# A two-layer encoder on one core: giving every split-weight buffer its own start remainder modulo 512 bytes

## The chip, the core and the metric

The kernel runs on one core of a Trainium2 chip. Its engines work side by side and hand work to each other through semaphores: TensorE (PE in the views; PEld is its weight load), VectorE (DVE), ScalarE (ACT), GpSimd (POOL) and SyncE (SP), which issues the loads from device memory. SBUF is the on-chip memory from which they read their operands, 128 partitions wide; an address here is a byte offset along a partition. The metric is the device time of one execution in microseconds.

## What is computed

The reference is a trunk of two layers on an input of 512 tokens by 1024 features in float32. Cut to what matters:

```python
for i in range(2):
    h = rms_norm(x, mix_pre_g[i])
    if i == 0: m = ssd_mixer(h, ...)        # w_in (1024 x 6176), scan over chunks, w_out (2048 x 1024)
    else:      m = shortconv_mixer(h, ...)  # w_in (1024 x 3072), conv of 3, w_out (1024 x 1024)
    x = x + rms_norm(m, mix_post_g[i])
    f = conv_ffn(rms_norm(x, ffn_pre_g[i]), ...)   # w_up (1024 x 5632), conv of 3, w_down (2816 x 1024)
    x = x + rms_norm(f, ffn_post_g[i])
```

Nearly all of the arithmetic is in these matrix products.

## The kernel before

**Split operands.** Every large product is made of three matmuls in the type float32r. Each float32 operand is split into a high part and a low part (the rest), and the three products high x high, high x low, low x high are summed in one PSUM bank. The activations are kept in split form: `h_hi` and `h_lo`, `y_hi` and `y_lo`, `hid_hi` and `hid_lo`.

**Weight units.** The weights come in 228 units of 128 x 1024 elements, numbered `u`. SyncE loads a unit into one of two raw buffers `w_raw`. ScalarE copies it to `w_hi` (line 355), VectorE writes the difference to `w_lo` (line 585), and TensorE reads both. The function `splits_to(end)`, one on ScalarE and one on VectorE, does the splits up to a unit, and the calls to it are written by hand between the other work of the two engines. A unit's pair of buffers is a slot. The 48 units of the first layer's input product use three slots; from unit `U_OUT` = 48 on there are five, and the 180 units there take them in turn:

```python
def slot(u):
    return u % 3 if u < U_OUT else (u - U_OUT) % SLOTS
```

ScalarE may split unit `u` when the unit that had the slot before is done on TensorE (`before(u)`, semaphore `unit_done`). Slots 3 and 4 lie in memory that the first layer's scan used, so their first use waits for the scan instead: on `seg_done` for slot 3 and on `scan_done` for slot 4.

**Two ways of using a unit.** In the function `unit` (lines 849 to 851, through `three`) the weights are the stationary operand, 128 x 128 at a time, and the activations move through, 512 columns in one matmul; `half_unit` does the same with 256 columns, for three units after each of three of the four output products. In `project` (lines 910 to 912) the activations are stationary and 512 columns of the weights move. Either way one unit takes 24 matmuls of 512 columns (48 of 256 in a half unit), and every matmul has a weight load of its own. TensorE's order of work is fixed in its block and has no slack of its own.

**Where operands begin.** The tensors are allocated one behind another. The sizes of nearly all per partition are multiples of 512 bytes, and in the built program all the large operands (`x_tok`, `h_hi`, `h_lo`, `w_raw`, all ten `w_hi`/`w_lo`, `hid_hi`, `hid_lo`, `feat`, `pad`) begin at the same remainder modulo 512 bytes. The slices that TensorE takes of them are at multiples of 512 bytes too. VectorE's and ScalarE's accesses are not all so: the convolution reads `pad[:, f % 2, tap:tap + T]` for taps 0, 1 and 2 (line 645), thus at 0, 4 and 8 bytes past a multiple of 512, and ScalarE writes the same buffer from element 3 on (line 406), 12 bytes past one.

Other lines that the views name: 1013 are the transposes of `feat`, 1020 and 1038 the float32 matmuls of the scan with its state, 1030 those with the mask (the last that `scan_done` counts), 1060 a sum over partitions with one moving column. These are float32, without a split.

Of the kernel before, what the change touches and what calls it, by code (L numbers as in the profile page):

```python
# [6 lines left out]
F32R = mybir.dt.float32r  # L7
# [3 lines left out]
P = 128  # L11
# [4 lines left out]
def build(nc, x, mix_pre_g, mix_post_g, ffn_pre_g, ffn_post_g, ssd_w_in, ssd_conv_w, ssd_conv_b,  # L16
          ssd_dt_bias, ssd_A_log, ssd_D, ssd_norm_w, ssd_w_out, sc_w_in, sc_conv_w, sc_w_out,
          ffn_w_up, ffn_conv_w, ffn_conv_b, ffn_w_down, out):
    _, T, D = x.shape
# [6 lines left out]
    GROUPS = 8  # L26
# [76 lines left out]
    U_OUT = len(SOURCES)  # L103
# [18 lines left out]
    def slot(u):  # L122
        return u % 3 if u < U_OUT else (u - U_OUT) % SLOTS

    def before(u):

        if u < U_OUT + 3:
            return u - 3 if u >= 3 else None
        return u - SLOTS if u >= U_OUT + SLOTS else None
# [22 lines left out]
    with ctx:  # L152
        def sb(name, shape, dt=F32, stack=ctx):
            return stack.enter_context(nc.sbuf_tensor(name, shape, dt))

        def sem(name):
            return ctx.enter_context(nc.semaphore(name))
# [3 lines left out]
        x_tok = sb("x_tok", [P, C, D])  # L161
        h_hi, h_lo = sb("h_hi", [P, DT, T], F32R), sb("h_lo", [P, DT, T], F32R)
        w_raw = sb("w_raw", [P, 2, D])
        w_hi = [sb(f"w_hi{n}", [P, D], F32R) for n in range(3)]
        w_lo = [sb(f"w_lo{n}", [P, D], F32R) for n in range(3)]
        ident, tri = sb("ident", [P, P]), sb("tri", [P, P])
        par = sb("par", [P, 4, P])

# [43 lines left out]

        with ExitStack() as rest:

            for n in (3, 4):
                w_hi.append(sb(f"w_hi{n}", [P, D], F32R, rest))
                w_lo.append(sb(f"w_lo{n}", [P, D], F32R, rest))
            g_row = sb("g_row", [P, D], stack=rest)
            r_row = sb("r_row", [P, 2, T], stack=rest)

            with ExitStack() as at_boundary:
                scaled = sb("scaled", [P, 2, D], stack=at_boundary)
            cpad = sb("cpad", [P, T + P], stack=rest)
            acc, gated, side = (sb(n, [P, T], stack=rest) for n in ("acc", "gated", "side"))
            hid_hi, hid_lo = sb("hid_hi", [P, FT, T], F32R, rest), sb("hid_lo", [P, FT, T], F32R, rest)
# [17 lines left out]
        evicted, seg_done, exps_done, conv_step, silu_done = (  # L243
            sem(n) for n in ("evicted", "seg_done", "exps_done", "conv_step", "silu_done"))
# [97 lines left out]
        def _(act):  # L342
            split_at = [0]

            def splits_to(end):

                for u in range(split_at[0], min(end, U_END)):
                    act.wait_ge(raw_landed[u % 2], 16 * (u // 2 + 1))
                    if before(u) is not None:
                        act.wait_ge(unit_done, before(u) + 1)  # L350
                    elif u == U_OUT + 3:
                        act.wait_ge(seg_done, GROUPS)
                    elif u == U_OUT + 4:
                        act.wait_ge(scan_done, GROUPS)
                    nc.scalar.activation(w_hi[slot(u)][:], w_raw[:, u % 2, :], ACT.Copy).then_inc(w_hi_done, 1)  # L355
                    split_at[0] = u + 1
# [11 lines left out]
            for k in range(DT):  # L368
                act.wait_ge(xn_turned, k + 1)
                nc.scalar.activation(h_hi[:, k, :], bank[k % 6][:], ACT.Copy, scale=one(col_gain(MIX_PRE, 0, k))).then_inc(h0_hi_done, 1)  # L370
                if k == 0:
                    act.wait_ge(wdt_landed, 16)
                    act.wait_ge(wdt_cleared, 2)
                    nc.scalar.activation(wdt_hi[:, :, 0:HEADS], wdt_raw[:], ACT.Copy).then_inc(wdt_split, 1)
                if k == 3:
                    splits_to(1)
            splits_to(2)
            act.wait_ge(dt_row_mm, 1)
            nc.scalar.copy(dt_row[:], bank[7][0:HEADS, :]).then_inc(dt_row_done, 1)
# [11 lines left out]
            act.wait_ge(dt_act, 3)  # L391
            nc.scalar.activation(dt_e[:], dt_e[:], ACT.Ln, bias=1.0).then_inc(dt_act, 1)
            splits_to(3)
            act.wait_ge(acs_mm, 1)
            nc.scalar.copy(acs_row[:], bank[2][0:HEADS, :]).then_inc(acs_row_done, 1)
# [34 lines left out]
            for g in range(GROUPS):  # L430
# [25 lines left out]
                for j in range(XG):  # L456
                    n = XG * g + j
# [679 lines left out]
```

## Time and profile before

| | |
|---|---|
| median of three runs | 1345.62 us (1345.48 to 1346.71) |
| the profiled execution | 1345.41 us |
| its span, first to last instruction | 1343.7 us |
| PE busy | 1332.0 us, 99% |
| PEld busy | 1115.5 us, 83% |
| DVE busy | 784.3 us, 58% |
| ACT busy | 569.2 us, 42% |
| DMA | 101 GB/s on average |
| granted TensorE clock | 1.000 of full speed |

Busy shares are of the span. A matmul's record is longer than the step from one matmul's start to the next one's, since they are pipelined; so the duration of one is not what it costs. What it costs is the step between starts, called the pitch below.

### The profile page before, as it was taken

The numbers are of one execution on the slowest core, as the hardware profiler recorded it, in microseconds if no ns is written. First come the engines' busy times: TensorE is split into PE (matmuls) and PEld (weight loads), VectorE is DVE, ScalarE is ACT, GpSimd is POOL, SyncE is SP. The second block draws the span as 40 slices with busy tenths as digits, with TensorE's granted clock in tenths as the row PEclk, the third lists the DMA queues.
The fourth block names the chain that finished last, engine by engine and source line by source line (L and its number), as shares of the span: only waits on it lengthen the run. The fifth ranks groups of instructions, "written<-read, shape, count | busy, mean of one in ns | idle before, by whom it ended". The sixth has DMA issues, their size and how long they took to land.

```text
span 1343.7 us, 15929 instructions
## 1 busy us (share of the span) xinstructions
PE 1332.0 (99%) x6474; PEld 1115.5 (83%) x6474; DVE 784.3 (58%) x1139; ACT 569.2 (42%) x875; POOL 24.8 (2%) x28
## 2 busy tenths in 40 slices
PE   8999999999999999999999999999999999999998
PEld 7888888888888988888888888888898888888886
DVE  4889888888525566656542265445566666654223
ACT  6666655566316434333331173222554433333112
POOL 0000000000000000000000000000000000000000
PEclk9999999999999999999999999999999999999999
DMA  5533233432231233333333313334223333333331
GB/s 151 161 110 92 84 107 110 125 110 90 94 125 54 79 95 109 99 103 96 95 125 112 101 55 94 94 99 128 72 69 106 109 94 96 104 99 126 96 108 63
DMA packets 181773, 135.70 MB, mean 101 GB/s; under 512 B 5645, under 2 KB 169893, under 8 KB 180677
## 3 DMA queue, kind: packets, MB, share of 16 engines
q1 hardware_dynamic: 181653, 134.62, 32.8%
q8 instruction: 51, 0.84, 0.2%
q14 instruction: 21, 0.17, 0.0%
q10 hardware_dynamic: 48, 0.07, 0.0%
HBM read 132.51 MB, written 2.16 MB: 100 GB/s over the span
## 4 chain that ended last, share of the span: by engine, by line
PE 97%; ACT 1%; issue 0%; DVE 0%; DMA 0%; SPq 0%; DVEq 0%; ACTq 0%
PE bank L849 21%; PE bank L851 21%; PE bank L850 21%; PE bank L910 9%; PE bank L911 9%; PE bank L912 9%; PE bank L1030 1%; PE bank L1038 1%; PE bank L1020 1%; PE bank L887 1%; PE bank L1013 1%; PE bank L1002 0%; DMA pages<-in_ssd_norm_w 0%; ACT w_hi L355 0%; ACT h_hi L370 0%
## 5 line engine op out<-in xcount | busy, mean ns | idle before, releaser
L849 PE MATMUL bank<-h_hi,w_hi 128*128 128x512 f32 (+1 forms) x1352 | 513.8, 380 | 0.0
L851 PE MATMUL bank<-h_lo,w_hi 128*128 128x512 f32 (+1 forms) x1352 | 511.1, 378 | 0.0
L850 PE MATMUL bank<-h_hi,w_lo 128*128 128x512 f32 (+1 forms) x1352 | 510.8, 378 | 0.0
L585 DVE TENSOR_TENSOR w_lo<-w_raw,w_hi 128x1024 fp32r<-128x1024 f32 x228 | 286.0, 1257 | 325.8 <-ACT w_hi L355 325.8
L355 ACT ACTIVATE w_hi<-w_raw 128x1024 fp32r<-128x1024 f32 x228 | 238.4, 1053 | 195.3 <-PE bank L912 172.3
L851 PEld LDWEIGHTS bank<-h_lo,w_hi 128*128 128x128 f32 x1352 | 254.2, 188 | 47.4
L850 PEld LDWEIGHTS bank<-h_hi,w_lo 128*128 128x128 f32 x1352 | 254.4, 188 | 46.6
L849 PEld LDWEIGHTS bank<-h_hi,w_hi 128*128 128x128 f32 x1352 | 254.3, 188 | 46.4
L910 PE MATMUL bank<-w_hi,hid_hi 128*128 128x512 f32 x416 | 162.4, 390 | 0.0
L912 PE MATMUL bank<-w_hi,hid_lo 128*128 128x512 f32 x416 | 161.9, 389 | 0.0
L911 PE MATMUL bank<-w_lo,hid_hi 128*128 128x512 f32 x416 | 161.8, 389 | 0.0
L912 PEld LDWEIGHTS bank<-w_hi,hid_lo 128*128 128x128 f32 x416 | 78.1, 188 | 16.3
L910 PEld LDWEIGHTS bank<-w_hi,hid_hi 128*128 128x128 f32 x416 | 78.1, 188 | 16.1
L911 PEld LDWEIGHTS bank<-w_lo,hid_hi 128*128 128x128 f32 x416 | 78.1, 188 | 15.9
L780 DVE SCALAR_TENSOR_TENSOR acc<-cpad,par,acc 128x512 f32<-128x512 f32 x104 | 77.9, 749 | 4.4 <-ACT acc L542 1.8
L645 DVE SCALAR_TENSOR_TENSOR feat<-pad,par,feat 128x512 f32<-128x512 f32 x96 | 71.5, 751 | 13.6 <-ACT feat L407 11.3
L546 ACT ACTIVATE acc<-acc 128x512 f32<-128x512 f32 x44 | 27.9, 634 | 115.8 <-DVE acc L780 115.8
L542 ACT ACTIVATE acc<-cpad,par 128x512 f32<-128x512 f32 x44 | 35.9, 817 | 81.9 <-DVE cpad L793 81.9
L549 ACT ACTIVATE hid_hi<-gated 128x512 fp32r<-128x512 f32 x44 | 27.8, 633 | 81.2 <-DVE gated L802 81.2
L785 DVE TENSOR_TENSOR hid_lo<-gated,hid_hi 128x512 fp32r<-128x512 f32 x52 | 36.0, 693 | 36.4 <-ACT hid_hi L549 30.8
L910 PE MATMUL bank<-w_hi,y_hi 128*128 128x512 f32 x128 | 50.3, 393 | 0.0
L912 PE MATMUL bank<-w_hi,y_lo 128*128 128x512 f32 x128 | 49.9, 390 | 0.0
(146 smaller groups left out, 943.9 us busy)
## 6 DMA issues: line engine op xcount, KB each, us to landing
w_raw<-in_ffn_w_up SPq DMA_DIRECT2D x88, 512.0 KB, 3.7
w_raw<-in_ssd_w_in SPq DMA_DIRECT2D x48, 512.0 KB, 3.9
w_raw<-in_ffn_w_down SPq DMA_DIRECT2D x44, 512.0 KB, 3.5
w_raw<-in_sc_w_in SPq DMA_DIRECT2D x24, 512.0 KB, 3.7
acs_b<-acs_dram SPq DMA_DIRECT2D x8, 1024.0 KB, 6.1
w_raw<-in_ssd_w_out SPq DMA_DIRECT2D x16, 512.0 KB, 3.5
w_raw<-in_sc_w_out SPq DMA_DIRECT2D x8, 512.0 KB, 3.5
x_tok<-in_x SPq DMA_DIRECT2D x4, 512.0 KB, 4.9
```

The costliest lines, as they stand in the source:

```text
L355: nc.scalar.activation(w_hi[slot(u)][:], w_raw[:, u % 2, :], ACT.Copy).then_inc(w_hi_done, 1)
L542: nc.scalar.activation(acc[:], cpad[:, CW - 1:CW - 1 + T], ACT.Identity, bias=one(col_ffn_b(layer, t)), scale=one(col_ffn_w(layer, CW - 1, ...
L585: nc.vector.tensor_tensor(w_lo[slot(u)][:], w_raw[:, u % 2, :], w_hi[slot(u)][:].bitcast(F32), ALU.subtract).then_inc(w_lo_done, 1)
L645: nc.vector.scalar_tensor_tensor(out=feat[:, f, :], in0=pad[:, f % 2, tap:tap + T], scalar=one(col_ssd_w(tap, page_tile)), in1=feat[:, f, ...
L780: nc.vector.scalar_tensor_tensor(out=acc[:], in0=cpad[:, tap:tap + T], scalar=one(cols(tap)), in1=acc[:], op0=ALU.mult, op1=ALU.add).then_ ...
L785: nc.vector.tensor_tensor(hid_lo[:, t, :], gated[:], hid_hi[:, t, :].bitcast(F32), ALU.subtract).then_inc(hid_lo_done, 1)
L849: nc.tensor.matmul(dst, wh, xh, start=start, stop=False)
L850: nc.tensor.matmul(dst, wl, xh, start=False, stop=False)
L851: return nc.tensor.matmul(dst, wh, xl, start=False, stop=stop)
L910: nc.tensor.matmul(dst[:], in_hi[:, k, toks], hi, start=k == 0, stop=False)
L911: nc.tensor.matmul(dst[:], in_hi[:, k, toks], lo, start=False, stop=False)
L912: last = nc.tensor.matmul(dst[:], in_lo[:, k, toks], hi, start=False, stop=k == b.tiles - 1)
```

## The change

The buffers of the split weights are no longer tensors of their own but views into two larger tensors, `w_split` for slots 0 to 2 and `w_split_rest` for slots 3 and 4. A view is shifted by a number of bytes of its own, so that each of the ten parts begins at another remainder modulo 512 bytes, counted from the remainder at which the other operands begin:

| slot | high part | low part |
|---|---|---|
| 0 | 128 | 256 |
| 1 | 384 | 16 |
| 2 | 448 | 192 |
| 3 | 8 | 160 |
| 4 | 480 | 320 |

Each of the two tensors is 512 bytes longer than its parts, so all tensors behind them move by a multiple of 512 bytes and keep their remainders. With the shift the part of slot 4 reaches past the memory of the mask, and slot 3's low part into it, so slot 3's first use now waits on `scan_done` too.

```diff
-        w_hi = [sb(f"w_hi{n}", [P, D], F32R) for n in range(3)]
-        w_lo = [sb(f"w_lo{n}", [P, D], F32R) for n in range(3)]
+
+        w_split = sb("w_split", [P, 6 * D + P], F32R)
+
+        def part(src, nth, shift):
+            return src[:, nth * D + shift // 4:(nth + 1) * D + shift // 4]
+
+        w_hi = [part(w_split, 1, 128), part(w_split, 4, 384), part(w_split, 5, 448)]
+        w_lo = [part(w_split, 3, 256), part(w_split, 0, 16), part(w_split, 2, 192)]
...
-            for n in (3, 4):
-                w_hi.append(sb(f"w_hi{n}", [P, D], F32R, rest))
-                w_lo.append(sb(f"w_lo{n}", [P, D], F32R, rest))
+            w_split_rest = sb("w_split_rest", [P, 4 * D + P], F32R, rest)
+            w_hi += [part(w_split_rest, 0, 8), part(w_split_rest, 3, 480)]
+            w_lo += [part(w_split_rest, 1, 160), part(w_split_rest, 2, 320)]
...
-                    elif u == U_OUT + 3:
-                        act.wait_ge(seg_done, GROUPS)
-                    elif u == U_OUT + 4:
+                    elif u >= U_OUT + 3:
                         act.wait_ge(scan_done, GROUPS)
```

No engine gets an instruction more or less, and none changes its place. The one wait that changes stands in ScalarE's row at the end of the last scan group, where it has written the last two pieces of `y_hi` and their squares. Before:

```order
L459 ACTIVATE y_hi<-feat,par 128x512 [waits y_step]
L462 ACTIVATE square<-feat 128x512 [waits summed]
L355 ACTIVATE w_hi3<-w_raw 128x1024 [waits seg_done,raw_landed1]
L355 ACTIVATE w_hi4<-w_raw 128x1024 [waits scan_done,raw_landed0]
L562 ACTIVATE small<-bank5 128x4 [waits y_sum_mm]
```

And after the change, at the same place:

```order
L463 ACTIVATE y_hi<-feat,par 128x512 [waits y_step]
L466 ACTIVATE square<-feat 128x512 [waits summed]
L359 ACTIVATE w_split_rest<-w_raw 128x1024 [waits scan_done,raw_landed1]
L359 ACTIVATE w_split_rest<-w_raw 128x1024 [waits scan_done,raw_landed0]
L566 ACTIVATE small<-bank5 128x4 [waits y_sum_mm]
```

The rows stand as they stood; only the semaphore ahead of slot 3's first use is another, and all line numbers from there on are four or more higher.

## Rows read from the trace of the kernel before

**Rows 1.** The page: busy time of TensorE, and the chain that ended last.

```profile
PE 1332.0 (99%) x6474; PEld 1115.5 (83%) x6474; DVE 784.3 (58%) x1139; ACT 569.2 (42%) x875; POOL 24.8 (2%) x28
...
PE 97%; ACT 1%; issue 0%; DVE 0%; DMA 0%; SPq 0%; DVEq 0%; ACTq 0%
```

**Rows 2.** TensorE's waits, first and last of five: total us, times, longest.

```profile
PE bank L855 <- POOL tri L330: 1.8, 1, 1.8
...
PE bank L1013 <- ACT feat L413: 0.2, 1, 0.2
```

**Rows 3.** TensorE's groups by shape: count, busy us, mean ns, idle us before.

```profile
L849 PE MATMUL bank<-h_hi,w_hi 128*128 128x512 f32 x1208 | 472.8, 391 | 0.0
...
L910 PE MATMUL bank<-w_hi,hid_hi 128*128 128x512 f32 x416 | 162.4, 390 | 0.0
...
L910 PE MATMUL bank<-w_hi,y_hi 128*128 128x512 f32 x128 | 50.3, 393 | 0.0
...
L849 PE MATMUL bank<-h_hi,w_hi 128*128 128x256 f32 x144 | 41.0, 285 | 0.0
```

**Rows 4.** One stretch of 512-column matmuls: busy (count), granted clock, DMA share, GB/s.

```profile
460.00:780.00 320.00, 320.00 (x1413) 1.00 0.34 104
```

**Rows 5.** Timeline of TensorE, half units, first and last of nine matmuls.

```profile
442.76 0.28 PE L850 MATMUL bank<-h_hi,w_lo 128*128 128x256 f32 x1
...
443.72 0.28 PE L849 MATMUL bank<-h_hi,w_hi 128*128 128x256 f32 x1
```

**Rows 6.** The chain in order of time, float32 groups: start us, us, what.

```profile
92.28 0.87 PE bank L1013 x8
...
98.63 1.29 PE bank L1020 x6
...
355.08 0.89 PE bank L1060 x8
```

**Rows 7.** Weight loads by shape: split operands, and float32 of the scan.

```profile
L850 PEld LDWEIGHTS bank<-h_hi,w_lo 128*128 128x128 f32 x1352 | 254.4, 188 | 46.6
...
L1038 PEld LDWEIGHTS bank<-feat,prev 128*128 128x128 f32 x96 | 11.3, 191 | 2.7 <-issue 2.7
```

**Rows 8.** Timeline of TensorE at the start of a unit behind the transposes.

```profile
132.96 0.39 PE L850 MATMUL bank<-h_hi,w_lo 128*128 128x512 f32 x1
133.19 0.40 PE L851 MATMUL bank<-h_lo,w_hi 128*128 128x512 f32 x1
133.42 0.40 PE L849 MATMUL bank<-h_hi,w_hi 128*128 128x512 f32 x1
133.66 0.39 PE L850 MATMUL bank<-h_hi,w_lo 128*128 128x512 f32 x1
133.88 0.39 PE L851 MATMUL bank<-h_lo,w_hi 128*128 128x512 f32 x1
...
135.26 0.39 PE L851 MATMUL bank<-h_lo,w_hi 128*128 128x512 f32 x1
```

**Rows 9.** By line: duration ns min/median/max of the convolution and the splits.

```profile
L645 DVE SCALAR_TENSOR_TENSOR feat<-pad,par,feat x96: 737/752/755, 32.8 to 327.0; 128x512 f32<-128x512 f32 x96
...
L406 ACT COPY pad<-bank x32: 566/586/592, 31.4 to 324.1; 128x512 f32<-128x512 f32 x32
...
L585 DVE TENSOR_TENSOR w_lo<-w_raw,w_hi x228: 1215/1226/2318, 17.2 to 1312.1; 128x1024 fp32r<-128x1024 f32 x114
```

**Rows 10.** Timeline: unit 0's low part, and TensorE's first use of it.

```profile
17.20 1.22 DVE L585 TENSOR_TENSOR w_lo<-w_raw,w_hi 128x1024 fp32r<-128x1024 f32 x1
...
20.61 0.39 PE L849 MATMUL bank<-h_hi,w_hi 128*128 128x512 f32 x1
```

**Rows 11.** Timeline: the last scan matmuls, and the splits into slots 3, 4.

```profile
338.36 1.97 PE L1030 MATMUL bank<-mask,xdt 128*64 128x128 f32 x32
...
348.60 1.99 ACT L355 ACTIVATE w_hi<-w_raw 128x1024 fp32r<-128x1024 f32 x2
```

## The prediction

> **What bounds the kernel now.** I read the busy shares and the chain first: TensorE is busy for 1332.0 of 1343.7 us, and 97% of the chain that ended last is its own work [rows 1]. Its list of waits has five entries, the longest 1.8 us, and neither split is among them [rows 2]; the large groups have 0.0 us of idle time before them [rows 3]. So the time is a number of matmuls times the step between their starts (the pitch), and the change can matter in three places: the pitch, a split that comes too late, and the altered wait.
>
> How many: 3 lines x 1208, 3 x 416 and 3 x 128 matmuls of 512 columns, together 5256, and 3 x 144 = 432 of 256 columns [rows 3]. Every one of the 5688 reads a part of the split weights, as stationary or as moving operand.
>
> What one costs: 1413 in 320 us, 226.5 ns [rows 4], in a stretch that holds units and output products alike. The count takes in the matmuls that the edges cut, so I take 226.7. With 256 columns the pitch is 0.96 us / 8 = 120 ns [rows 5]. The difference, 106.7 ns for 256 columns, is 0.417 ns per column, one tick of the 2.4 GHz clock that is granted throughout (1.00 in [rows 4]). What is left is a fixed 13.3 ns per matmul, at 256 and at 512 columns alike. These products make 5256 x 226.7 + 432 x 120 = 1243 us of the span.
>
> **The change part by part.** It removes and adds no instruction, so the sum has one term that could be large: 5256 times whatever the pitch moves by. One nanosecond is 5.3 us, or 0.4%.
>
> *The pitch.* No TensorE operand of the trace begins at another remainder than the rest in a split product, so the price is not shown, and I bound it from both sides.
>
> For a gain: is the fixed 13.3 ns a collision between the weight load and the moving stream, which begin at the same remainder today? The float32 groups are the nearest rows. 128 columns take 0.87/8 = 109 ns and 256 take 1.29/6 = 215 ns [rows 6], 0.83 ns per column and only some 2 ns fixed, although they too load 128 weights for each matmul and begin at the same remainders. With one moving column the pitch is 0.89/8 = 111 ns [rows 6]: that is the weight load alone, so neither 227 nor 120 ns is set by it. If all of the difference between 13.3 and 2 ns were a collision that the shifts end, the gain would be 11.3 x 5688 = 64 us. Against it speaks the load's own record: 188 ns beside the fast stream of the split products, 191 ns beside the slow one of line 1038 [rows 7]. Two streams that got into each other's way would make the load longer beside the faster one, and it isn't.
>
> For a loss: behind the transposes the pitch is not yet 226.7. From 132.96 us the starts are 230, 230, 240, 220 ns apart and so on, ten steps in 2.30 us, a mean of 230 ns [rows 8], and then it settles. The same happens after each float32 group. So the pitch depends on something beside the number of columns, on how load and stream stand to each other in time, and it has a state in which it stays. By the starts, which the view rounds to 10 ns, these steps lie between 220 and 240 ns. If the remainders are part of that state, a weight part that changes its remainder from matmul to matmul (high, low, high) could keep it from settling: 230 instead of 226.7 is +3.3 ns, times 5256, +17 us.
>
> For none: within a unit the slices move by 512 and 2048 bytes, high and low parts change, and weights are stationary in one half of the work and moving in the other; the pitch is 226.7 in all of them [rows 3, 4]. That excludes a dependence on the address above 512 bytes, not one below. VectorE, ScalarE and the loads use the same memory all the while (0.34 of the DMA engines' time in [rows 4]) without a trace in the pitch. If accesses that come at any moment and any address don't disturb the stream, a fixed address relation is not likely to either. I take 0 for the pitch, as the row of load durations is the one that speaks to a collision most directly.
>
> The Trainium skill (TensorE: Matmul & The Clock Gate, "Step-by-step: what each phase is for") says that TensorE has two independent SBUF read ports, so loading the next weights takes no read bandwidth from the running matmul. By that rule the sum stays at 1345.6 us and the gain of 64 us can't exist; the trace agrees in the load's 188 and 191 ns and leaves the 13.3 ns unexplained.
>
> *Slot 3's high part* begins 8 bytes past a multiple of 16, the only one of the ten. Slot 3 has 180 / 5 = 36 units, and 16 of a unit's 24 matmuls read the high part: 576 matmuls. Nothing in the trace shows TensorE at such a start. The bounds are nothing, and the half rate of the float32 stream, 0.83 - 0.417 ns for each of 512 columns, +213 ns x 576 = +123 us. VectorE reads at starts of 0, 4 and 8 bytes, and its 96 convolution steps lie between 737 and 755 ns [rows 9], so a start inside 16 bytes costs that engine at most 2.4%. I take nothing here.
>
> The Trainium skill (SBUF — State Buffer, "Specifications (TRN2)" and its note on cachelines) has 16-byte lines with a penalty for each crossing. By it a shifted 512-column operand touches 129 lines and not 128; at four columns' time, 1.7 ns, this would be an estimate of +1 us in all. No row here shows it.
>
> *The splits.* ScalarE now writes, and VectorE reads and writes, at other starts. Bounds: nothing, and the spread of accesses that are off by 4, 8 or 12 bytes: 18 ns of 752 for VectorE and 592 - 566 = 26 ns for ScalarE [rows 9], scaled to a split of twice the length some 35 and 50 ns. The tightest place I found is the first unit: its low part is done at 18.42 us and TensorE begins it at 20.61, 2.19 us later [rows 10]. So 85 ns more for the pair is hidden behind TensorE's work. Were the cover gone everywhere, it would be 228 x 0.085 = 19 us, but for that a split would have to grow from 1.23 us to over 3.
>
> *The wait.* ScalarE gets to slot 3's first split at 348.60 us; the matmuls that `scan_done` counts end at 338.36 + 1.97 = 340.33 [rows 11]. The wait is over 8.3 us before it is reached. Behind it in ScalarE's row stand slot 4's split, which waited on the same semaphore already, and the copy for line 1060. Cost 0.
>
> *Sum.* 1343.7 us of span, 1.7 us around it, and four terms at 0: 1345.4 us for the profiled execution, which lies 0.2 under the median of the runs. I forecast the median, 1345.6.
>
> **The rivals.**
>
> A, the forecast, no change: 1345.6 us.
>
> B, slower: the stream doesn't settle. Place: all split matmuls. Price +3.3 ns each, 1363 us; with every step at the longest of [rows 8], 240 ns, +70 us. It decides from 0.5 ns on, since 5256 x 0.5 = 2.7 us is 0.2%. For it speaks that the pitch has such states at all [rows 8], and that the present one is at their low end. Against it: the state is found again after every disturbance, at whatever address.
>
> C, faster: the parallel remainders cost something now. All of it gone is 1281 us; a state halfway between today's 226.7 and the shortest step of [rows 8], 220 ns, is -3.3 x 5256 = -17 us, 1328 us. For it: the fixed 13.3 ns against 2 ns [rows 5, 6]. Against it: [rows 7].
>
> D, slower: slot 3's start inside 16 bytes. From nothing to +123 us; at 5 ns a matmul it would be +3 us and just visible.
>
> E: the change does nothing to the remainders that matter, because only the distance of high and low part counts or only whole blocks do. That is A's time.
>
> **How the numbers follow.** A with E 0.64, B 0.16, C 0.14 (0.08 for all of it, 0.06 for a part), D and a late split together 0.06. A measurement of this kernel tells 0.2% from no change; the three runs lie within 0.09%. Faster 0.14, same 0.64, slower 0.22. The range takes in A, B at its likely size and the small form of C: 1328 to 1366 us; outside are C in full, and B and D beyond 20 us, less than 0.2 together.
>
> **What would show it.** In the profile after, TensorE's count in 460 to 780 us says all: 1413 is A, some 1391 is B, over 1425 is C. In the timeline the starts should lie 227 and 226 ns apart with any slot's weights, and slot 3's high part like the others (D: two of three steps longer in every fifth unit). The load's 188 ns should stay. The subtract's median should stay within 35 ns of 1226 and the copy's within 50 of its own, with no new wait in TensorE's list. I am wrong if the pitch depends on how operands stand to each other below 512 bytes, which nothing in this trace could test.

## The result: 1.8% slower, by a longer step between matmuls

| | median | runs |
|---|---|---|
| before | 1346.16 us | 4 (1345.48 to 1347.25) |
| changed | 1369.55 us | 4 (1369.28 to 1370.03) |

The ratio is 1.0177, with an interval from 1.0165 to 1.0189. The change costs 23.4 us; the likeliest forecast was no change, and the range ended at 1366.

The page of the changed kernel, busy time and chain, answers to [rows 1]:

```profile
PE 1356.9 (99%) x6474; PEld 1117.1 (82%) x6474; DVE 784.7 (57%) x1139; ACT 568.8 (42%) x875; POOL 24.8 (2%) x28
...
PE 97%; DVE 1%; ACT 1%; issue 0%; DMA 0%; DVEq 0%; ACTq 0%
```

The same 6474 matmuls keep TensorE busy 24.9 us longer, while the sums of the weight loads, VectorE and ScalarE moved by 1.6 us at most. So the added time is TensorE's own work. Its list of waits, first and last of five, answers to [rows 2]:

```profile
PE bank L859 <- POOL tri L336: 1.8, 1, 1.8
...
PE bank L1017 <- ACT feat L417: 0.2, 1, 0.2
```

Neither split's line (359, 589) is in it. The stretch of [rows 4], in the changed kernel (PE, PEld, DVE, ACT and POOL busy with counts, then clock, DMA share, GB/s):

```profile
460.00:780.00 320.00, 320.00 (x1383) 259.59 (x1382) 161.76 (x191) 106.89 (x129) 0.00 (x0) 1.00 0.34 100
```

It has 1383 matmuls where there were 1413, at the same granted clock: 231.4 ns per matmul. The timeline of TensorE in one unit of it, which should be read as [rows 8] was, by the distances between starts:

```profile
496.87 0.40 PE L853 MATMUL bank<-h_hi,w_split 128*128 128x512 f32 x1
497.11 0.39 PE L854 MATMUL bank<-h_hi,w_split 128*128 128x512 f32 x1
497.33 0.40 PE L855 MATMUL bank<-h_lo,w_split 128*128 128x512 f32 x1
497.57 0.40 PE L853 MATMUL bank<-h_hi,w_split 128*128 128x512 f32 x1
497.81 0.40 PE L854 MATMUL bank<-h_hi,w_split 128*128 128x512 f32 x1
498.04 0.39 PE L855 MATMUL bank<-h_lo,w_split 128*128 128x512 f32 x1
```

This is far behind any stall, and the starts are still 0.22 to 0.24 us apart. In the kernel before, steps of this length stood behind a float32 group and ended after ten [rows 8]; here they last.

**Where the time is.** I worked out the mean step, from each split matmul's start to the next start on TensorE, in both traces, which hold nanoseconds. The few steps that span a wait or a change of work are in it, so the mean before is 227.8 and not 226.7:

| | count | before | changed | difference |
|---|---|---|---|---|
| units, 512 columns | 3624 | 227.8 ns | 232.4 ns | +16.8 us |
| output products, 512 columns | 1631 | 227.5 ns | 232.5 ns | +8.2 us |
| half units, 256 columns | 432 | 120.4 ns | 119.0 ns | -0.6 us |

The sum is +24.4 us, against +23.9 in the spans (1367.6 and 1343.7). The other matmuls take 0.4 us less.

### The profile page after: what moved, and what is told of

Same layout as the page of the kernel before. It is cut to its first block, busy times and chain, and to the rows that moved or that the text cites. A ratio compares the mean times of both kernels' runs of the same rounds, so it can differ in the third digit from the quotient of the medians.

```text
span 1367.6 us, 15929 instructions
## 1 busy us (share of the span) xinstructions
PE 1356.9 (99%) x6474; PEld 1117.1 (82%) x6474; DVE 784.7 (57%) x1139; ACT 568.8 (42%) x875; POOL 24.8 (2%) x28
## 4 chain that ended last, share of the span: by engine, by line
PE 97%; DVE 1%; ACT 1%; issue 0%; DMA 0%; DVEq 0%; ACTq 0%
PE bank L853 21%; PE bank L854 21%; PE bank L855 21%; PE bank L914 9%; PE bank L916 9%; PE bank L915 9%; PE bank L1034 1%; PE bank L1042 1%; PE bank L1024 1%; PE bank L891 1%; PE bank L1017 0%; DVE feat L649 0%; PE bank L1006 0%; DMA x_tok<-in_x 0%; DVE w_split L589 0%
## 5 line engine op out<-in xcount | busy, mean ns | idle before, releaser
L853 PE MATMUL bank<-h_hi,w_split 128*128 128x512 f32 (+1 forms) x960 | 371.9, 387 | 0.0
L854 PE MATMUL bank<-h_hi,w_split 128*128 128x512 f32 (+1 forms) x960 | 369.0, 384 | 0.0
L855 PE MATMUL bank<-h_lo,w_split 128*128 128x512 f32 (+1 forms) x960 | 368.4, 384 | 0.0
L589 DVE TENSOR_TENSOR w_split<-w_raw,w_split 128x1024 fp32r<-128x1024 f32 x156 | 198.1, 1272 | 201.1 <-ACT w_split L359 201.1
L359 ACT ACTIVATE w_split<-w_raw 128x1024 fp32r<-128x1024 f32 x156 | 163.6, 1053 | 120.9 <-PE bank L916 103.9
L855 PEld LDWEIGHTS bank<-h_lo,w_split 128*128 128x128 f32 x960 | 180.7, 188 | 38.9
L853 PEld LDWEIGHTS bank<-h_hi,w_split 128*128 128x128 f32 x960 | 180.5, 188 | 37.2
L854 PEld LDWEIGHTS bank<-h_hi,w_split 128*128 128x128 f32 x960 | 180.3, 188 | 37.0
L853 PE MATMUL bank<-h_hi,w_split_rest 128*128 128x512 f32 (+1 forms) x392 | 147.5, 376 | 0.0
L854 PE MATMUL bank<-h_hi,w_split_rest 128*128 128x512 f32 (+1 forms) x392 | 147.3, 376 | 0.0
L855 PE MATMUL bank<-h_lo,w_split_rest 128*128 128x512 f32 (+1 forms) x392 | 146.8, 375 | 0.0
L914 PE MATMUL bank<-w_split,hid_hi 128*128 128x512 f32 x248 | 98.0, 395 | 0.0
L915 PE MATMUL bank<-w_split,hid_hi 128*128 128x512 f32 x248 | 97.4, 393 | 0.0
L853 PEld LDWEIGHTS bank<-h_hi,w_split_rest 128*128 128x128 f32 x392 | 73.6, 188 | 14.7
L854 PEld LDWEIGHTS bank<-h_hi,w_split_rest 128*128 128x128 f32 x392 | 73.6, 188 | 14.0
```

Source lines behind the costliest of these rows:

```text
L589: nc.vector.tensor_tensor(w_lo[slot(u)][:], w_raw[:, u % 2, :], w_hi[slot(u)][:].bitcast(F32), ALU.subtract).then_inc(w_lo_done, 1)
L853: nc.tensor.matmul(dst, wh, xh, start=start, stop=False)
L854: nc.tensor.matmul(dst, wl, xh, start=False, stop=False)
L855: return nc.tensor.matmul(dst, wh, xl, start=False, stop=stop)
L914: nc.tensor.matmul(dst[:], in_hi[:, k, toks], hi, start=k == 0, stop=False)
L915: nc.tensor.matmul(dst[:], in_hi[:, k, toks], lo, start=False, stop=False)
```

## Experiments

Two theories stood first. R: the pitch follows the remainders, by the difference between the stationary and the moving operand. A: it rises because the remainder changes from one matmul to the next. There are two kinds of kernels here: variants of the whole kernel, and section kernels, in which TensorE alone runs rows of split-type matmuls with chosen remainders. A section's settled pitch is worked out from the starts in its trace, over the steps behind the first 14. Remainders are counted, here as in the change, from the one at which all large tensors begin.

### The layout and the wait alone

```diff
+        w_hi = [part(w_split, n, 0) for n in range(3)]
+        w_lo = [part(w_split, n + 3, 0) for n in range(3)]
```

and the same for `w_split_rest`; all else as in the changed kernel.

> The changed kernel with all ten shifts set to 0: the two large tensors, the extra 512 bytes and the altered wait stay, the remainders are those of before. Theory R (the pitch depends on the remainders, by the difference between weight load and moving stream) and theory A (it depends on the remainder changing from one matmul to the next) both expect the time of before, 1346 us, with a pitch of 226.7 ns. A rival, that the layout or the wait costs the 23 us, expects 1369 us.

Measured: 1345.65 us, ratio 1.0000 (0.9991 to 1.0009). The larger tensors and the wait on `scan_done` cost nothing; all of the loss hangs on the ten shifts.

### All parts shifted by 256 bytes, and the low parts alone

```diff
+        w_hi = [part(w_split, n, 256) for n in range(3)]     # second kernel: 0
+        w_lo = [part(w_split, n + 3, 256) for n in range(3)]
```

> All ten parts shifted by the same 256 bytes. Theory A: no remainder changes from matmul to matmul, so the pitch settles at 226.7 ns and the time is 1346 us. Theory R: every weight load is now 256 bytes apart from its moving stream, so the pitch is another one, anywhere between 224 and 236 ns, 1332 to 1395 us, and not 1346.

> High parts unshifted, low parts shifted by 256 bytes, so the remainder changes in every group of three matmuls. Theory A: the pitch doesn't settle and stays near 231 ns, 1363 to 1372 us. Theory R: one load (or one stream) in three differs, so the shift against before is about a third of that of the kernel with all parts at 256.

Measured: 1346.18 us (ratio 1.0004, 0.9995 to 1.0014) and 1345.43 us (0.9997, 0.9988 to 1.0007). Both are the kernel before. Alternating 0 and 256 costs nothing, against theory A; but a constant 256 costs nothing either, which theory R as I had written it did not allow. Either R is wrong, or the period is 256 bytes and not 512. The sections told which.

### A sweep of remainders

```python
for i in range(45): nc.tensor.matmul(bank[i % 4][:, 0:512], s((0, 0, 0)[i % 3]), m((64, 64, 64)[i % 3], 512), start=True, stop=True)
```

> No part of the reference is computed: TensorE alone runs 52 sections of 45 split-type matmuls, each section with its own remainders of the stationary and the moving operand, parted by eight float32 matmuls; the output is a copy of the input. Theory R: sections with a constant difference between the two remainders have a pitch of their own for each difference, and equal remainders (16/16 to 384/384) have 226.7 ns like 0/0. Theory A: all sections with constant remainders settle at 226.7 ns, and only those in which the remainder alternates lie near 231 ns. A start inside 16 bytes (4 and 8): theory D of the prediction expects a longer pitch there alone.

The timeline of TensorE, five of the sections with their whole length (the moving operand at 0, 4, 8, 64 and 128 bytes, the stationary at 0):

```profile
16.43 10.48 PE L59 MATMUL bank<-moved,still 128*128 128x512 f32 x45
...
28.45 10.89 PE L61 MATMUL bank<-moved,still 128*128 128x512 f32 x45
...
40.88 10.74 PE L63 MATMUL bank<-moved,still 128*128 128x512 f32 x45
...
77.67 10.56 PE L69 MATMUL bank<-moved,still 128*128 128x512 f32 x45
...
102.05 10.74 PE L73 MATMUL bank<-moved,still 128*128 128x512 f32 x45
```

The same 45 matmuls take 10.48 us at equal remainders and up to 10.89 elsewhere; at 128 bytes they take 0.26 us more, which over 44 steps is 6 ns each. Settled pitches in ns, 512 columns:

| difference in bytes | moving shifted | stationary shifted |
|---|---|---|
| 0, 256 | 226.7 | 226.7 |
| 4 | 236.7 | - |
| 8 | 233.3 | 230.7 |
| 16 | 231.5 | 233.3 |
| 32 | 233.4 | 233.3 |
| 64 (also moving 320) | 228.9 | 233.3 |
| 128 | 233.3 | 232.3 |
| 192 (also 448) | 233.3 | 228.9 |

Equal remainders of 64, 128, 256 or 384 on both sides gave 226.7 ns. So a constant remainder doesn't settle at 226.7 unless it is the same on both sides modulo 256, and a remainder that alternates by 256 does: theory A falls, theory R stands with a period of 256 bytes. Stationary shifted by 192 gives the 228.9 ns of moving shifted by 64, as a difference should. Not as expected: equal remainders of 16 gave 230.0 ns, and moving shifted by 384, which is 128 modulo 256, gave 232.3 ns and not 233.3. The start of 4 bytes has the longest pitch, 236.7 ns, as rival D would have it, but the start of 8 bytes, 233.3, is no longer than that of 32. Alternating loads (0, b, 0) lay at 231.1 to 233.3 ns for b of 8 to 128.

### The slots of the changed kernel, section by section

> Again no part of the reference is computed: TensorE runs sections of 45 matmuls each and the output is a copy of the input. The first ten sections use the remainders of the changed kernel's slots 0 to 4 in the order high, low, high, as stationary and then as moving operand, the other side at 0. Theory R (the pitch is set by the difference of the two remainders modulo 256): the settled pitches lie between 228 and 236 ns and their mean, over units and output products as the kernel has them, is near 231.2, the 226.7 of before and the 23.4 us over 5256 matmuls. Further sections: differences in steps of 8 to 16 bytes, equal remainders on both sides (226.7 ns if they are multiples of 64), 256 columns, and bfloat16, where no theory has a number; if the stream of four-byte columns is what collides, two-byte columns show no dependence.

| slot (high, low) | as stationary | in the kernel's units | as moving |
|---|---|---|---|
| 0 (128, 256) | 233.3 | 233.1 | 228.9 |
| 1 (384, 16) | 232.2 | 232.8 | 232.8 |
| 2 (448, 192) | 228.9 | 229.1 | 233.3 |
| 3 (8, 160) | 231.9 | 231.8 | 232.2 |
| 4 (480, 320) | 231.2 | 231.6 | 232.2 |

The third column is the mean step in the changed kernel's five-slot stages, from its own trace, without the few steps over 300 ns. The five slots differ by 4 ns there, and the sections give each of them within 0.7 ns. The kernel's output products weren't split by slot; taken together they lie at 231.9 ns without those steps, the mean of the last column. The mean of all ten sections is 231.7, where 231.2 was expected. So the remainders account for the loss.

Further sections: no difference between 8 and 240 bytes was under 226.7 ns (the lowest were 228.9 at 12 and at 64). Equal remainders gave 226.7 ns at 32, 96 and 192, 231.1 at 8, 48 and 80, and 237.8 at 4. While the stationary start was a multiple of 32, a difference of 64 gave 228.9 ns from wherever it was counted (0, 32, 64 or 128). From a stationary start of 16 it did not; the section with 16 and 80 bytes is the second line, behind one with 32 and 96:

```profile
446.11 10.55 PE L139 MATMUL bank<-moved,still 128*128 128x512 f32 x45
...
458.21 10.45 PE L141 MATMUL bank<-moved,still 128*128 128x512 f32 x45
```

It settled at 226.7 ns, although the two remainders differ. So the difference alone sets the pitch only between starts at multiples of 32; elsewhere the position counts too. And bfloat16, two of its eight sections in the timeline, with the moving operand at 0 and at 128 bytes:

```profile
526.89 9.66 PE L159 MATMUL bank<-moved,still 128*128 128x512 bf16 x44
...
561.38 9.66 PE L165 MATMUL bank<-moved,still 128*128 128x512 bf16 x44
```

All eight have 215.8 or 215.9 ns: the moving operand at 0, 32, 64, 128, 192 and 256, the stationary one at 64, and both at 16.

### The difference, tested in the whole kernel

All parts at 128, at 192 and at 64, as in the diff for 256 above with that number; and, with all parts at 128, the six activation operands moved too:

```diff
+        def moved(name, n, stack=ctx):
+            src = sb(name, [P, n * T + P], F32R, stack)
+            return src[:, 32:32 + n * T].rearrange("p (n t) -> p n t", n=n)
+
+        h_hi, h_lo = moved("h_hi", DT), moved("h_lo", DT)
...
+                y_hi, y_lo = moved("y_hi", IT, late), moved("y_lo", IT, late)
...
+            hid_hi, hid_lo = moved("hid_hi", FT, rest), moved("hid_lo", FT, rest)
```

> All ten parts shifted by 128 bytes. Theory R with the section pitches: units 3624 x (232.3 - 226.7) = +20 us, output products 1632 x (233.3 - 226.7) = +11 us, half units -1 us: 1376 us. Theory A (only a change from matmul to matmul costs): 1346 us.

> As the kernel with all parts at 128, and the six activation operands (h, y, hid, high and low) shifted by 128 bytes as well, so the difference between weight load and moving stream is 0 again. Theory R: 1346 us. Rival, the weights' own remainder or that of the base counts: 1376 us as without the second shift.

> All ten parts shifted by 192 bytes. The sections gave 228.9 ns with the load 192 ahead and 233.3 ns with the stream 192 ahead. Theory R: units 3624 x 2.2 = +8 us, output products 1632 x 6.7 = +11 us, half units -1 us: 1364 us, and in the trace the output products alone at 233.3 ns. If only the size of the shift counted, both would have the same pitch.

> All ten parts shifted by 64 bytes, the mirror of the shift by 192. The sections gave 233.3 ns with the load 64 ahead and 228.9 ns with the stream 64 ahead. Theory R: units 3624 x 6.7 = +24 us, output products 1632 x 2.2 = +4 us, half units -3 us: 1370 us. If the direction didn't matter: 1362 us as with 192.

| weights | activations | expected | measured | ratio (95%) |
|---|---|---|---|---|
| 128 | 0 | 1376 | 1374.55 | 1.0216 (1.0201 to 1.0232) |
| 128 | 128 | 1346 | 1345.29 | 0.9998 (0.9989 to 1.0008) |
| 192 | 0 | 1364 | 1362.33 | 1.0125 (1.0108 to 1.0142) |
| 64 | 0 | 1370 | 1372.21 | 1.0198 (1.0184 to 1.0212) |

The same two stretches in each trace, one with units alone and one with an output product in most of it (length, then PE busy with count, clock, DMA share, GB/s). Before:

```profile
480.00:620.00 140.00, 140.00 (x619) 1.00 0.33 98
660.00:780.00 120.00, 120.00 (x531) 1.00 0.33 110
```

Weights at 128:

```profile
480.00:620.00 140.00, 140.00 (x602) 1.00 0.34 98
660.00:780.00 120.00, 120.00 (x516) 1.00 0.33 108
```

Weights and activations at 128:

```profile
480.00:620.00 140.00, 140.00 (x619) 1.00 0.34 98
660.00:780.00 120.00, 120.00 (x531) 1.00 0.35 110
```

Weights at 192:

```profile
480.00:620.00 140.00, 140.00 (x614) 1.00 0.34 99
660.00:780.00 120.00, 120.00 (x518) 1.00 0.34 108
```

Weights at 64:

```profile
480.00:620.00 140.00, 140.00 (x602) 1.00 0.34 98
660.00:780.00 120.00, 120.00 (x524) 1.00 0.34 106
```

The counts say it without any arithmetic. Shifting the activations by as much as the weights brings back 619 and 531. And 192 costs the units little (614) and the output product much (518), while 64 does the reverse (602 and 524): in a unit the weights are the stationary side, in an output product the moving one, so the sign of the difference turns over. For these starts, all multiples of 64, it is the difference that counts, with its sign.

But not the difference alone. With weights at 64 the time is 2 us over what was expected. Two stretches of that kernel, both mostly of an output product on `hid` with the same remainders, the second product and the last:

```profile
700.00:780.00 80.00, 80.00 (x351) 1.00 0.33 108
1250.00:1330.00 80.00, 80.00 (x344) 1.00 0.36 114
```

The first three output products have steps of 229.0 to 229.2 ns, the last one 233.3 throughout its 527 steps; 4.3 ns x 527 is 2.3 us, the whole miss. One pair of remainders has lasted at two pitches in one kernel.

### Slot 3's start inside 16 bytes

```diff
-            w_hi += [part(w_split_rest, 0, 8), part(w_split_rest, 3, 480)]
+            w_hi += [part(w_split_rest, 0, 0), part(w_split_rest, 3, 480)]
```

> The changed kernel with slot 3's high part at 0 and not at 8 bytes, so that all ten starts are multiples of 16. Rival D (a start inside 16 bytes carries a part of the loss): at least 3 us under the changed kernel's 1369.6 us. Theory R: slot 3 stays at a mixed pitch between 229 and 234 ns, within 3 us of 1369.6.

Measured: 1370.56 us (ratio to before 1.0184, 1.0169 to 1.0200), 1.0 us above the changed kernel; the two intervals overlap. Slot 3's mean step in the units is 233.3 ns with (0, 160) against 231.8 with (8, 160). Rival D is refuted for 8 bytes in this kernel: the odd start is no worse than its neighbours. The edit changes slot 3's difference to the activations together with its place inside 16 bytes. The sections with equal remainders part the two: there 8 bytes (231.1 ns) cost no more than 16, 48 and 80 (230.0 to 231.1), which are multiples of 16. A start 4 bytes past such a multiple can be worse: 236.7 ns moving at 4, 236.0 at 20, 237.8 with both at 4.

### A version that uses a difference: the half units 64 bytes ahead

The 256-column sections have another order: 120.0 ns at equal remainders, 113.3 with the load 64 ahead.

The diff, cut; 16 elements are 64 bytes, and `D + 64` elements a multiple of 256 bytes:

```diff
+        HALVES = {b.end + n for b in back if b.pre for n in range(AHEAD)}
+        ROOM = D + 64
...
+            at = nth * ROOM + (16 if u in HALVES else 0)
```

> The kernel before, with each weight part at a multiple of 256 bytes from the others, except that the nine units that go through half_unit (256 columns) lie 64 bytes further. The sections gave 113.3 ns with the load 64 ahead against 120 ns at equal remainders. Theory R: 432 x 6.7 = -2.9 us, 1342.6 us. If half units in the kernel are set by something else: 1345.5 us.

Measured: 1343.95 us against 1345.50 for the kernel before, ratio 0.9989 (0.9980 to 0.9998). It is the fastest kernel of the study, by 0.1%, at the edge of what can be told. The direction is right, the size is half: the mean step of its half units is 117.0 ns, not 113.3, against 120.4 before; 3.4 ns x 432 is 1.5 us, all of the gain. In each of the three stages the first 48 steps have a mean of 113.7 ns; behind the transposes that follow, the other steps lie at 117.8.

### Is the fixed part the load's reads?

```python
for i in range(45): nc.tensor.matmul(bank[i % 4][0:32, 0:512], still[:, 0:32], m(0, 512), start=True, stop=True)
```

> No part of the reference is computed; sections of 45 split-type matmuls with 128, 96, 64 and 32 loaded columns, with 128 to 512 moving columns, and with a start of 16 bytes on both sides. If the fixed part of the pitch (13.3 ns at equal remainders) is a collision between the load's reads and the stream's, it shrinks with the loaded columns: near 10, 7 and 3 ns for 96, 64 and 32, and so does its dependence on the remainders. If it is a fixed cost of changing weights, it stays at 13.3 ns.

The timeline of the sections with 32 loaded columns, the moving operand at 0, 64 and 128:

```profile
163.60 10.66 PE L83 MATMUL bank<-moved,still 128*32 128x512 f32 x45
...
175.80 10.64 PE L85 MATMUL bank<-moved,still 128*32 128x512 f32 x45
...
187.98 10.63 PE L87 MATMUL bank<-moved,still 128*32 128x512 f32 x45
```

Settled pitches for 128, 96, 64 and 32 loaded columns at equal remainders: 226.7, 230.1, 230.0 and 231.7 ns. The fixed part doesn't shrink with the load; it grows a little. At 32 columns the four remainders tried give 230.7 to 231.7 ns, at 128 columns 226.7 to 233.3. Over the four remainders 0, 64, 128 and 192 the pitches spread by 6.6, 3.3, 2.7 and 1.0 ns with 128, 96, 64 and 32 loaded columns. So a shorter load takes away most of the dependence, as the collision would have it, and not the fixed cost. My reading of the 13.3 ns as reads of the load that push the stream aside is refuted. With 320 moving columns all four differences gave 146.7 ns, one tick per column and again 13.3; with 384 three gave 173.3 and 128 bytes 176.0; with 448 they gave 200.0 to 204.0, the shortest at a difference of 64 (202.7 at equal remainders). With 128 moving columns all four gave 111.6 or 111.7. So equal remainders are the best case at 512 columns, and not at every length. With the stationary start at 16 the moving ones at 16, 48, 112 and 144 gave 231.1 to 233.5 ns, and that at 208 gave 226.7, where a difference of 192 from a multiple of 32 costs 233.3.

### Whose operands meet?

```python
for i in range(60): nc.tensor.matmul(bank[i % 4][:, 0:512], s([0, 128][i % 2]), m([128, 0][i % 2], 512), start=True, stop=True)
```

> No part of the reference is computed; sections of 60 split-type matmuls whose two remainders both change from matmul to matmul. Theory N (the stream of a matmul meets the weight load of the next one): with the moving remainder equal to the next matmul's stationary one the pitch settles at 226.7 ns, and with it equal to its own it lies between 228 and 236. Theory O (a matmul's own two operands count): the reverse. If only changing or not changing counts, neither settles. The last sixteen sections repeat four constant pairs behind a single matmul of 128 to 400 columns: if the same pair settles at more than one pitch, the start decides between states, and a pitch from one section holds for the kernel only within that spread.

| stationary in turn | moving equal to its own | moving equal to the next stationary |
|---|---|---|
| 0, 128 | 228.4 | 230.0 |
| 0, 64 | 231.9 | 233.3 |
| 0, 192 | 231.5 | 233.3 |
| 0, 32 | 231.6 | 230.0 |
| 0, 64, 128 | 229.9 | 233.3 |
| 0, 96, 192 | 231.1 | 228.9 |
| 0, 128, 64 | 232.4 | 232.7 |

Neither settles at 226.7 ns: theories N and O both fail. Nor does the moving remainder equal to the stationary one before it (232.6, 233.3 and 231.8 ns in the three rows of three). When both sides change from matmul to matmul, being equal in pairs is not enough.

The last sections repeat one pair (moving at 192, 256 columns) behind one matmul of 128, 200, 300 and 400 columns; the timeline of TensorE:

```profile
299.88 7.04 PE L96 MATMUL bank<-moved,still 128*128 128x256 f32 x60
...
308.63 7.25 PE L99 MATMUL bank<-moved,still 128*128 128x256 f32 x60
...
317.65 6.97 PE L102 MATMUL bank<-moved,still 128*128 128x256 f32 x60
...
326.42 7.00 PE L105 MATMUL bank<-moved,still 128*128 128x256 f32 x60
```

The second is longer: it settled at 117.8 ns, the three others at 113.3. One pair of remainders has two lasting states, and what runs ahead of the row can change which one it finds. It isn't known what picks it: behind the same eight float32 matmuls this pair settled at 113.3 ns in one section kernel and at 117.8 in another. The half-unit kernel's 113.7 and 117.8 ns are nearly the same two values, so half of its gain is missing because most of its steps lie in the longer state. With 512 columns, equal remainders found 226.7 ns from all four starts, a difference of 64 found 228.9, and one of 128 found 232.2, 232.3 or 233.4.

## Why the prediction was wrong

**What bounds the kernel** was right: the matmul count times the pitch, and a nanosecond of pitch worth 5.3 us.

**The pitch** is the step that failed: "I take 0 for the pitch". The measured term is +4.6 ns on 3624 and +5.0 ns on 1631 matmuls, +25 us. Two arguments led there, and one against it was passed over. The record of the load, 188 and 191 ns [rows 7], was taken as the row that speaks to a collision most directly. It does not: the load's busy time stayed within 2 us in all while the pitch rose by 2%, so that record doesn't see the effect. That accesses of other engines "at any moment and any address don't disturb the stream" was carried over to a fixed relation of TensorE's own two operands, and that was wrong. The sentence "That excludes a dependence on the address above 512 bytes, not one below." was right, and should have weighed more, since the change lies entirely below. The last line of the prediction names this as what would make it wrong. The Trainium skill's rule of two independent read ports (TensorE: Matmul & The Clock Gate, "Step-by-step: what each phase is for") gave 1345.6 us; the runs with all parts at 128, with and without the activations, show that stationary and moving operand do matter to each other in this type, by 29.3 us, so here the measurement decides against what I took from the rule.

**Rival B** had the place and the direction: all split matmuls, longer steps. It was priced at +3.3 ns from the ten steps of [rows 8], and the measured rise is 4.6 to 5.0; that mis-sized term, 17 us for 25, put the result 3.6 us outside the range. Its mechanism was wrong. The reason, "a weight part that changes its remainder from matmul to matmul", falls because all parts at a constant 128 cost more (1374.55 us) than the mixture. And the stream does settle, at a longer pitch: with the stationary start constant at 64 the steps are 233 or 234 ns. That the steps behind a stall have about the same length isn't shown to have the same cause.

**Rival C**, that equal remainders cost something today, is refuted at 512 columns: in 20 or more differences none was under 226.7 ns. It holds at 256 columns (1.5 us in the half-unit kernel), which I did not forecast. Its price rested on a misreading as well. The program has four transposes where [rows 6] shows x8: a float32 matmul leaves two records, so 109 ns is the step of a record and not the time of 128 columns. And 109 ns is no more than the 111 ns of the group with one column, so the load may set both; split matmuls of 128 columns take 111.7 too. The "2 ns fixed" against which the 13.3 were held isn't shown, nor is the slope of 0.83 ns per column, on which D's bound of +123 us stands too.

**Rival D** is not supported: taking the 8 bytes away did not help. The estimate of +1 us, worked out from the 16-byte lines of the Trainium skill (SBUF — State Buffer, "Specifications (TRN2)"), isn't supported either: without the 8 bytes the time was 1.0 us more, not less. **Rival E**, that the change misses what matters, is refuted by the 23 us.

**The splits** cost nothing, as said. Both kinds of slot, in VectorE's subtract after the change (min/median/max):

```profile
L589 DVE TENSOR_TENSOR w_split<-w_raw,w_split x156: 1215/1225/2315, 17.0 to 1324.4; 128x1024 fp32r<-128x1024 f32 x156
L589 DVE TENSOR_TENSOR w_split_rest<-w_raw,w_split_rest x72: 1212/1225/1227, 353.9 to 1335.6; 128x1024 fp32r<-128x1024 f32 x72
```

The median is 1 ns under that of [rows 9], so VectorE's subtract doesn't show the starts. ScalarE's copy has medians of 1053 and 1046 ns, against 1047 before. **The wait** cost nothing, shown by the kernel with all shifts at 0.

**What stays open** is the cause in the hardware. Shown are the dependence on the signed difference modulo 256 bytes between starts at multiples of 32, a further dependence on the place elsewhere, both in float32r and absent in the bfloat16 sections, and several lasting states for one pair. Not shown is which two accesses meet, or whether any do: the fixed 13.3 ns don't follow the number of loaded columns while the dependence does, and equality in pairs with a matmul's own, the next or the previous load doesn't decide.

## What to carry to other kernels

Where float32r matmuls of 512 columns bound a kernel, let the stationary and the moving operand begin at the same remainder modulo 256 bytes, at a multiple of 32. Nearly all other layouts tried cost 1 to 5% of the pitch (16 with 80 and 16 with 208 cost nothing), and a kernel laid out like this one, in sizes that are multiples of 512 bytes, has the best case without trying. At 256 and 448 columns equal remainders are not the shortest, so measure them. Read the pitch from the starts, never from a record's duration. When a section kernel gives a pitch, repeat it behind other work before you count on it: one pair can have two. If a change touches a quantity that never varies in the trace, that trace gives no evidence that it is harmless.

## What the hardware showed unexpectedly

Float32r steps of 512 columns lie between 226.7 and 237.8 ns by the start remainders, at a granted clock of 1.00; bfloat16 is at 215.8 or 215.9 in all eight sections. With 256 columns the order is another: 120.0 ns at equal remainders, 113.3 to 120.0 elsewhere. With 320 columns no dependence was seen (146.7). A load of 32 columns costs no less than one of 128 (231.7 against 226.7 ns). The same pair of remainders can last at 113.3 or at 117.8 ns with 256 columns, and at 229.0 or at 233.3 ns with 512, within one kernel.
